# First mixer of a two-layer decoder step: decayed keys turned by 32x32 block transposes and a store, instead of TensorE transposes

## The reference, cut to what matters

```python
def step(s, inp):
    qc, kc, vc, gc = inp
    cum = jnp.cumsum(gc, axis=2)
    o_inter = jnp.einsum('bhtk,bhkv->bhtv', qc * jnp.exp(cum), s)
    ...
    o = o_inter + jnp.einsum('bhts,bhsv->bhtv', att, vc)
    last = cum[:, :, -1:, :]
    s_new = jnp.exp(last[:, :, 0, :])[..., None] * s + jnp.einsum(
        'bhsk,bhsv->bhkv', kc * jnp.exp(last - cum), vc)
    return s_new, o
```

## Time and profile before

| | |
|---|---|
| median of 3 runs | 1508.76 us (1508.12 to 1510.18) |
| profiled execution, its own time | 1508.85 us |
| its span | 1507.1 us |
| busy: PE, DVE, ACT, POOL | 98%, 66%, 45%, 28% |
| chain of waits that ended last: PE, DVE, ACT | 86%, 6%, 4% of the span |
| first mixer, heads 0 to 7 | about 53 to 602 us |
| last pair and end of the second mixer | about 1335 to 1507 us |

### The profile page before, as it was taken

One profiled execution on the slowest core, in us unless ns is written; L12 is line 12 of the kernel. 1 busy time (PEld: TensorE's weight loads), 2 busy tenths in 40 slices (PEclk: granted clock), 3 DMA queues, 4 the chain that ended last, 5 costly groups with the idle time before them and its releaser, 6 DMA issues.

```text
span 1507.1 us, 24074 instructions
## 1 busy us (share of the span) xinstructions
PE 1473.0 (98%) x8757; PEld 1083.9 (72%) x8757; DVE 1000.5 (66%) x1995; ACT 670.8 (45%) x1364; POOL 416.5 (28%) x335
## 2 busy tenths in 40 slices
PE   7999999999999999999999999999999999998998
PEld 6788888888888875445777777777777777764443
DVE  5878696978878684126467676768767667757321
ACT  4434545444444552212265555645555555545100
POOL 6012322121212100012051535344342625432200
PEclk9999999999999999999999999999999999999999
DMA  9985757767675734423236869696877879598731
GB/s 267 277 237 158 226 166 210 224 203 228 184 229 159 226 139 129 119 65 129 61 116 188 272 182 308 193 276 203 274 252 224 275 216 306 178 339 318 262 125 58
DMA packets 296267, 308.96 MB, mean 205 GB/s; under 512 B 26502, under 2 KB 252030, under 8 KB 296150
## 3 DMA queue, kind: packets, MB, share of 16 engines
q1 hardware_dynamic: 285014, 270.84, 58.9%
q0 software_dynamic: 11136, 36.59, 7.2%
HBM read 247.76 MB, written 126.73 MB: 248 GB/s over the span
## 4 chain that ended last, share of the span: by engine, by line
PE 86%; DVE 6%; ACT 4%; issue 2%; DMA 1%; POOL 0%; SPq 0%; DVEq 0%; POOLq 0%; ACTq 0%
PE psum L2179 44%; PE psum L2203 7%; PE psum L2692 7%; PE psum L2490 5%; PE psum L2516 4%; PE psum L2256 3%; PE psum L2142 2%; PE psum L2450 2%; PE psum L2548 2%; ACT psum L1307 1%; PE psum L2322 1%; PE psum L2267 1%; ACT psum L1316 1%; PE psum L2338 1%; PE psum L2342 1%
## 5 line engine op out<-in xcount | busy, mean ns | idle before, releaser
L2179 PE MATMUL psum<-arena 128*128 128x252 f32 (+1 forms) x3472 | 812.4, 385 | 2.4 <-DVE arena L1484 2.2
L2179 PEld LDWEIGHTS psum<-arena 128*128 128x128 f32 x3472 | 642.2, 190 | 124.4 <-issue 24.3
L985 POOL TENSOR_TENSOR arena<-arena 128x1024 f32<-128x1024 f32 x64 | 157.0, 2453 | 376.4 <-DMA arena<-k_pages 370.5
L1484 DVE TENSOR_TENSOR arena<-arena,psum 128x252 f32<-128x252 f32 (+1 forms) x310 | 129.2, 417 | 153.3 <-PE psum L2179 148.5
L2692 PE MATMUL psum<-arena 128*128 128x512 f32 x256 | 113.9, 598 | 1.6 <-DVE arena L1906 1.6
L2203 PE MATMUL psum<-arena 128*128 128x512 f32 x256 | 113.0, 595 | 0.1
L1060 ACT COPY arena<-psum 128x252 f32<-128x252 f32 (+1 forms) x124 | 46.2, 373 | 139.9 <-PE psum L2179 139.8
L2692 PEld LDWEIGHTS psum<-arena 128*128 128x128 f32 x256 | 47.2, 190 | 59.3 <-issue 56.9
L2203 PEld LDWEIGHTS psum<-arena 128*128 128x128 f32 x256 | 47.6, 191 | 57.3 <-issue 56.4
L1123 ACT ACTIVATE arena<-arena 128x1024 f32<-128x1024 f32 x48 | 50.6, 1055 | 85.4 <-DVE arena L1530 84.9
L1307 ACT ACTIVATE psum<-psum,arena 128x640 f32<-128x640 f32 (+3 forms) x64 | 58.9, 921 | 60.7 <-DVE arena L1839 60.7
(11 more groups left out here) (270 smaller groups left out, 2050.8 us busy)
## 6 DMA issues: line engine op xcount, KB each, us to landing
k_pages<-in_cache_k SPq DMA_DIRECT2D x64, 512.0 KB, 6.6
v_pages<-in_cache_v SPq DMA_DIRECT2D x64, 512.0 KB, 7.1
arena<-k_pages SPq DMA_DIRECT2D x64, 512.0 KB, 5.2
arena<-v_pages SPq DMA_DIRECT2D x64, 512.0 KB, 6.8
arena<-in_w_in_a SPq DMA_DIRECT2D x32, 512.0 KB, 7.1
arena<-in_x_prompt SPq DMA_DIRECT2D x16, 512.0 KB, 7.8
arena<-in_w_kv SPq DMA_DIRECT2D x16, 512.0 KB, 6.5
arena<-in_w_in_b SPq DMA_DIRECT2D x16, 512.0 KB, 7.5
```

The source lines that it names most:

```text
L985: pool.tensor_tensor(k_ring[:, m % 2], k_ring[:, m % 2], q_all[:, m % S:m % S + 1, :].broadcast_to([P, PAGES, P]), ALU.mult).then_inc(kq_m ...
L1484: dve.tensor_tensor(out, more, bank[n % 2][:, 0:size(u)], ALU.add).then_inc(of.by_dve, 1)
L2179: ins = pe.matmul(bank[n % 2][:, 0:size(u)], w[:, k, :], x[:, k, :], start=(k == 0 and r in (0, 1, 3, 4)), stop=(k == HK - 1), skip_group_ ...
```

## The change: what it does

1. **Decayed keys.** PE's transposes (L2305), ACT's copies (L1172) and the semaphores for them go. DVE turns `k_dec` by the same 32x32 block transposes as the values, into `k_blocks` (the place of `o_rs`), SP stores and loads it. `TOKEN_SETS` is 2: set 0 the values, set 1 the keys. `k_dec` now lies in `t1`. PE does the state's product as 32 products of 32 output rows each, in place of eight of 128, since the keys come back in four groups of 32.
2. **Order.** ACT makes exp(last - cum) after level 8. DVE makes and turns the keys after `merge(4)`, ahead of the samples' outer products. PE does the state's product after `fq(9)`, where it was ahead of `fq(8)`; DVE takes `fq(8)` ahead of `chunk_states(0)`, and copies `o_row` ahead of the gate.
3. **SP.** In heads 0 to 6: values out, values in, keys out, weights, keys in. In head 7: values out, keys out, values in, keys in, and then the second half of `w_o` and the rows of x. In head 7 DVE turns the values later, after `fq(1)`'s place.
4. **POOL** makes the F, Q sums for head h+2 at the end of head h (they were made at the start of head h+1), and waits for unit `fq(10)`, for the last of four also for `fq(12)`.
5. **Last pair.** DVE does `gate_in` behind `fin(p, 1)` and `shift(p - 1, 1)`, and `y_add(0, 1)` ahead of `smp_out` and `gate_smp`. PE does head 4 of `y_part(0)` one place earlier.

```diff
-TOKEN_SETS = 1
+TOKEN_SETS = 2
...
-        k_dec = logf[:, 0:T]
+        k_dec = t1[:, 0:T]
...
-        k_dec_tok = o_rs[:, 0:T].rearrange("p (t k) -> p t k", k=P)
+        k_blocks = o_rs[:, 0:T]
+        k_dec_tok = k_blocks.rearrange("p (g t l) -> p t g l", g=4, l=32)
...
             def tokens_in(h, n, blocks):
-                sp.wait_ge(rows_stored, STORES * token_set(h, n))
+                sp.wait_ge(rows_stored, STORES * token_set(h, TOKEN_SETS - 1 if h == AH - 1 else n))
...
                 if h < AH - 1:
                     tokens_out(h, 0, v_blocks)
+                    tokens_in(h, 0, v_blocks)
+                    tokens_out(h, 1, k_blocks)
                 sp.wait_ge(units.done, vg_unit(h, 14))
...
                 else:
                     for n in range(EARLY, AH - 2):
                         sp.dma_start(o_heads[n], o_dram[n]).then_inc(o_loaded, 16)
+                    tokens_out(h, 0, v_blocks)
+                    tokens_out(h, 1, k_blocks)
+                    tokens_in(h, 0, v_blocks)
+                tokens_in(h, 1, k_blocks)
+                if h + 1 == AH:
                     sp.dma_start(w_o[:, AH // 2:AH], w_o_rows[:, AH // 2:AH]).then_inc(w_o_loaded, 16)
                     res_in(0)
                     res_in(1)
-                    tokens_out(h, 0, v_blocks)
-                tokens_in(h, 0, v_blocks)
-                if h < AH - 1:
+                else:
                     sort_pages(sp, h + 1, 1)
...
             def head(h):
                 pool.dma_start(s_smp, state_in[h]).then_inc(state_loaded, 16)
-                if h + 1 < AH:
-                    if h:
-                        pool.wait_ge(units.done, fq_unit(h, 14))
-                    w_sums(h + 1, F, Q, sums_fq, fq_sums)
+                if h == 0:
+                    w_sums(1, F, Q, sums_fq, fq_sums)
...
                 pool.dma_start(prompt_out[h], s_all[:, NC - 1, :]).then_inc(prompt_stored, 16)
+                if h + 2 < AH:
+                    pool.wait_ge(units.done, fq_unit(h + 1, 11))
+                    w_sums(h + 2, F, Q, sums_fq, fq_sums, last_free=(units.done, fq_unit(h + 1, 13)))
...
                 level(8)
+                for t in range(NC):
+                    end = t * P if t >= NC // 2 else t * P + C - 1
+                    ins = act.activation(t1[:, cols(t)], cum[:, cols(t)], ACT.Exp, bias=cum[:, end:end + 1], scale=-1.0)
+                ins.then_inc(acts.sem, 1)
                 level(4)
...
-                for j in range(2):
-                    act.wait_ge(uu_done.sem, uu_done.at(f"turn{j}", h))
-                    act.copy(k_dec_tok[:, 4 * j:4 * j + 4, :], bank[4 + j][:, :]).then_inc(uu_taken_a, 1)
...
                 merge(4)
+                a("exp_kd")
+                dve.tensor_tensor(k_dec, k_h[:, 0:T], t1[:, 0:T], ALU.mult).then_inc(vecs.sem, 1)
+                dve.wait_ge(vecs.sem, vecs.at("k_dec", h))
+                turn_tokens(1, k_blocks, k_dec)
                 a("s_kept")
...
                 dve.wait_ge(s_all_free, h + 1)
+                fq(8)
                 chunk_states(0)
-                fq(8)
                 chunk_states(1)
...
-                gate_in(p)
+                if nxt:
+                    gate_in(p)
                 fin(p, 1)
                 kq(6)
                 if p:
                     shift(p - 1, 1)
+                if not nxt:
+                    gate_in(p)
...
+                last(0, 1)
                 if p:
                     smp_out(p - 1, 1)
                     gate_smp(p - 1)
                 vg(1)
-                last(0, 1)
...
-                v("k_dec")
-                for j in range(2):
-                    pe.wait_ge(uu_taken_v, 4 * h + 5 + j)
-                    for t in range(4 * j, 4 * j + 4):
-                        ins = pe.transpose(bank[4 + j][:, t % 4 * P:(t % 4 + 1) * P], k_dec[:, cols(t)], ident)
-                    ins.then_inc(uu_done.sem, 1)
...
-                fq(8, 9, 10)
+                fq(8, 9)
+                pe.wait_ge(pt_moved, MOVES * token_set(h, 1))
+                for j in range(2):
+                    pe.wait_ge(uu_taken_v, 4 * h + 5 + j)
+                    for c in range(4 * j, 4 * j + 4):
+                        for g in range(4):
+                            ins = pe.matmul(bank[4 + j][32 * g:32 * g + 32, c % 4 * P:(c % 4 + 1) * P], k_dec_tok[:, block_of(c), g],
+                                            v_tok[:, block_of(c)], start=True, stop=True, skip_group_check=True)
+                    ins.then_inc(uu_done.sem, 1)
+                fq(10)
```

More of the change, by code:

```diff
@@ L845, in _, with block_sums @@
             me = Steps(pool, w_steps)
-            def block_sums(one, two, out, done):
+            def block_sums(one, two, out, done, last_free=None):
                 me.did(pool.tensor_tensor(out[:, 0], two[:, 0:HK], two[:, HK:KT], ALU.add))
@@ L1159, in head @@
                 fq(2)
-                for t in range(NC):
-                    end = t * P if t >= NC // 2 else t * P + C - 1
-                    ins = act.activation(t1[:, cols(t)], cum[:, cols(t)], ACT.Exp, bias=cum[:, end:end + 1], scale=-1.0)
-                ins.then_inc(acts.sem, 1)
                 act.wait_ge(*units.taken(vg_unit(h, 13)))
@@ L2611, in pair @@
                 kq_n(5)
+                last((0, 4, 5))
                 scores(p, 4)
@@ L2618, in pair @@
                 kq_n(7)
-                last((0, 4, 6))
+                last((0, 5, 6))
                 new_score(p)
```

40 lines of the change are left out of this document (19 added, 21 removed).

## The result

| | before | after |
|---|---|---|
| median | 1509.47 us (4 runs, 1508.12 to 1511.8) | 1544.27 us (4 runs, 1542.39 to 1546.67) |
| profiled execution: time, span | 1508.85, 1507.1 us | 1542.85, 1541.0 us |
| ratio of after to before | | 1.023, 95% interval 1.0216 to 1.0243 |

The changed kernel is slower by 34.8 us. The forecast was +16.5, with a range that ended at 1536: the direction was right, the size less than half of it.

The account below looks back on a forecast made before the run. PE, busy for all of head 2's 67.6 us, was taken as the bound. Keys +4.4, head 7 +10.7, clock +3 and the rest -1.6 sum to +16.5 on 1508.85, so 1525.4 us, range 1507 to 1536.

Parts of the forecast that it names:

- part 5: The rest: F, Q sums moved on POOL, 0; last pair reordered, -1.6 us (0 to -3.8).
- the keys' lag: Time from the keys' first store to their load's landing on SP's queue, heads 0 to 6: taken as 14.5 us.
- Part 1: Heads 0 to 7: transposes gone, about 0.97 us less PE work per head; state's product costed at 0.
- Part 2: Heads 0 to 6: PE waits 1.6 us for the keys, +0.6 us a head, +4.4 in all (-6.8 to +16).
- Part 4: Behind head 7's wait of 10.8 us PE stays at the lower clock for a while: +3 us (0 to 3.3).
- Part 5, the F, Q sums at 0: POOL's sums moved to the end of the head before: 0, since POOL has time and their reader is half a head away.
- Part 3: Head 7: PE waits 10.8 us for w_o and 2.1 us more for the chunk states; sum +10.7 us.
- Part 5, the last pair: Moving y_add(0) ahead of seven small operations -1.3 us, moving gate_in -0.3; sum -1.6 us.
- The rivals: Keys in time, 1514, 0.2; weights slower, 1537 or more, 0.1; w_o hardly waited for, 1504.8, 0.13; w_o quick, keys late, 1516, 0.07.
- the slower one: Heads 0 to 6: weights slower than taken, keys' lag 16.2 us or more, 1537 us or more; chance 0.1.
- The signs: Expected in the profile: keys' waits of 1 to 3 us, heads 68.2 us apart, w_o wait 9 to 12, L2692's wait gone.

Follow-up runs that it names:

- experiment 8: Kernel of experiment 7, but with the F, Q sums at the changed kernel's place and waiting for DVE's gate step; 1507.28 us, ratio to before 0.9975.
- Experiment 1: Changed kernel with the keys' load issued ahead of the weights on SP's queue in heads 0 to 6; 1528.77 us, ratio to before 1.0125.
- experiment 3: Changed kernel with POOL's F, Q sums back at the start of a head; 1542.11 us, ratio to before 1.0217.
- experiment 9: Changed kernel with one more wait: POOL's F, Q sums start after DVE's gate step; 1542.05 us, ratio to before 1.0205.
- experiment 6: Kernel before with only y_add(0, 1) moved ahead of smp_out and gate_smp on DVE; 1508.83 us, ratio to before 0.9988.
- experiment 5: Changed kernel with gate_in and the y_part piece beside it put back as before in the last pair; 1547.66 us, ratio to before 1.0241.
- experiment 2: Changed kernel with w_o's second half and the two rows of x issued before head 7's stores; 1534.31 us, ratio to before 1.0166.
- experiment 4: Changed kernel with ten unused products of 512 columns on PE ahead of part(5)'s wait for w_o; 1544.78 us, ratio to before 1.023.
- experiment 7: Changed kernel with the edits of Experiment 1, experiment 2, experiment 3 and experiment 5 together; 1514.65 us, ratio to before 1.0026.
- experiment 10: Kernel before with the F, Q sums for head h+2 at the end of head h, behind its last unit and the gate step; 1509.24 us, ratio 0.9992.
- experiment 11: Kernel before with the F, Q sums at the end of the head, after unit 11 and DVE's gate step; 1510.56 us, ratio 1.0002.

## Why the prediction was right in direction and wrong in size

The step that failed most is in part 5: the F, Q sums at their new place were costed at 0 and gave PE 7.5 us of waits. After it come the keys' lag (+3.7 us), PE's own work (+2.8), the overlap (+2) and the clock (+1.7) that the table of the result lists.

- **Part 1, PE's own work: mis-sized.** Forecast -0.97 a head, measured -0.57 (67.62 to 67.05, head 2 of experiment 8, no waits in either). The transposes' 0.97 do go. But the state's product, costed at 0 by its duration (1.95 in both), moves from a step of 1.78 us to one of 1.88 (start to next start), and the six units that ran as one row of 10.86 us now run as 3.74 and 7.32: +0.2. The last 0.1 lies ahead of them; I didn't trace it. A duration includes what lies beside the next product; the step is what a head pays.
- **Part 2, the keys: the mechanism right, the lag short.** 14.5 us was taken between 14.5 and 16.2, and 15.7 was the mean. I had argued that the state's store would fill the weights' slow start; instead the issue of the weights grew to 6.46 us. The waits are 14.9 us in six heads, for 11.2 in seven. Experiment 1 gives them back.
- **Part 4 stopped at head 7.** It gave the clock to the wait of 10.8 us alone. A wait of 3.1 us in head 0 already cost 1.7, and experiments 3 and 9 show that the keys' waits can cost this in each head. In experiment 9 four more falls ate most of the 7.5 us.
- **Part 5, the F, Q sums at 0: the step that failed.** I asked whether POOL had time (52 of 67.6 us) and when the sums are read, not what DVE does beside them. The five waits behind the gate step are 7.5 us; experiments 3 and 9 move the adds and the waits go, and experiment 1 shows 1.8 us of head for each. The Trainium skill ("SBUF — State Buffer", Who interferes with whom) has the rule that a DVE instruction with two inputs in SBUF contends with a GpSimd instruction that reads SBUF; this case's traces agree (1.29 us without, 4.09 with the adds), and the forecast should have carried it. The profile of before had the sign as well: at the start of head 3 a scan takes 2.18 us beside an add of 2.14.
- **Part 3, head 7: right.** Wait for `w_o` 9.4 for 10.8, landing 9.2 us after the issue for 10.0, chunk states 2.4 for 2.1, slow products +2.75 for the +3 of part 4. Sum +12.7 for +13.7.
- **Part 5, the last pair: one term right, one too small to be read.** `y_add` -1.35 for -1.3, and experiment 6 has it alone. `gate_in`, forecast at -0.3, lies within the spread of experiment 5; that its wait would come back one item later is what the rows show (2.6 us before L2502). The profile has +0.8 through a load of pages that came later there than in the profile of before.
- **The rivals.** None was this case. The time of the slower one (1537 or more) holds the measured 1544, but by luck: its lag of 16.2 or more in every head was met in heads 0 and 3 alone, and the lag is the smaller part of the miss. What was missing was a rival with a new contention.
- **The signs.** PE's waits before the 32 products came in heads 0 to 5 as named, the wait for `w_o` was inside its 9 to 12 us, and L2692's wait went. The heads are 70.5 to 72.0 us apart from head 0's mark to head 5's, not 68.2.

## What to carry to other kernels

Before work of an idle engine is moved for nothing, list what the busy ones run beside the new place: POOL's adds beside a long DVE step with two inputs from SBUF cost it 2.8 us, where the same adds, started 0.15 us behind its end in experiment 8, cost it nothing. A load that PE will want goes ahead of a 2 MB load in the queue even if its data are ready late in the head; in experiment 1 nothing came to wait for the weights. And cost PE's work by the distance between starts, and a wait with what may follow it: 0.16 us of overlap, and 1.7 us if the clock falls.

## What the hardware did that I had not expected

- The granted clock fell to 0.50 after waits of PE of 2.3 to 3.3 us in five heads of experiment 9, and not after waits of 1.6 to 3.1 us in heads 1 to 5 of the changed kernel. A fall cost about 1.7 us.
- The wait of 2.42 to 2.43 us before the output's products of head 7 stands in nine profiles. In four of them (the changed kernel, experiments 1, 2 and 9) the clock stayed at 1.00 and they took 1.95 us, in five (3, 4, 5, 7, 8) it was down and they took 2.56 to 3.57. So the length of a wait alone doesn't tell here whether the clock falls.
- Where DVE's gate step and POOL's adds met, DVE's stretched by 2.8 us although it had begun 0.49 us ahead of the first add, and only the third add stretched, from 1.27 to 2.15 us. The logf step beside the adds took 3.09 us in experiment 3 and up to 3.69 in experiment 7, for 1.23.
- Where the order of PE and DVE up to that point was the same, the last pair still moved: the wait on the page's product at L2535 was 2.20 us before, and 3.48, 2.91 and 3.40 in experiments 6, 10 and 11. One profile of such a place is one draw.
